# Norms, scaled keys and decays of a gated delta-rule pair of heads are made at the end of the pair ahead; two groups of small operations go from VectorE to ScalarE

## What is computed

```python
q, k = l2norm(q), l2norm(k)               # per head, after a short causal convolution and silu
gam = jnp.cumsum(chunks(g), axis=-1)       # log decay
decay = jnp.exp(jnp.where(tril_incl, gam[..., :, None] - gam[..., None, :], -jnp.inf))
kk = jnp.einsum('bhnid,bhnjd->bhnij', k, k)
a_mat = jnp.where(tril_strict, beta[..., None] * kk * decay, 0.0)
sol = lax.linalg.triangular_solve(eye + a_mat, rhs, lower=True, unit_diagonal=True)
u, w = sol[..., :dv], sol[..., dv:]
def step(S, xs):                           # over the chunks
    u_c, w_c, qk_c, qd_c, kd_c, gl_c = xs
    v_new = u_c - w_c @ S
    o_c = qd_c @ S + qk_c @ v_new
    return S * gl_c + kd_c.T @ v_new, o_c
y = rms_norm(o, gdn_norm) * silu(z)        # then the output projection
```

## Time and profile before

| | |
|---|---|
| three runs | 2388.29, 2393.89, 2395.19 us; median 2393.89 us |
| profiled execution | 2386.92 us, its span 2385.1 us |
| TensorE busy in the span | 2271.2 us, 95% |
| VectorE, ScalarE, GpSimd busy | 1202.6, 996.0, 1128.9 us |
| delta-rule pairs, layer 0 | 121.9 to 447.5 us of the span |
| delta-rule pairs, layer 1 | 1299.5 to 1625.5 us of the span |
| TensorE idle in those two stretches | 56.2 us together |

### The profile page before, as it was taken

The page is one execution under the profiler, slowest core; times in us unless marked ns, Lnnn a source line. Parts: engine busy times, 40 slices in busy tenths (PEclk is TensorE's granted clock), DMA queues, the critical chain, the costliest instruction groups (busy, mean ns, idle before and its releaser), DMA issues.

```text
span 2385.1 us, 32695 instructions
## 1 busy us (share of the span) xinstructions
PE 2271.2 (95%) x12724; PEld 1854.7 (78%) x12724; DVE 1202.6 (50%) x2284; ACT 996.0 (42%) x2125; POOL 1128.9 (47%) x824
## 2 busy tenths in 40 slices
PE   6989997999999999999988999979999999999997
PEld 5677876788878888888766777867887888888886
DVE  4768778544442344440157778775445333444302
ACT  5545544455442333332265455445455224333222
POOL 4365366243345555554443564453443555555542
PEclk9999998999999999999989999989999999999998
DMA  4212111122233333333321111102222333333332
GB/s 138 62 45 58 54 47 39 52 74 75 72 87 97 97 93 97 97 97 98 97 63 58 45 54 54 56 26 67 76 76 67 96 97 93 96 97 96 97 97 84
DMA packets 98506, 183.34 MB, mean 77 GB/s; under 512 B 10928, under 2 KB 11056, under 8 KB 98224
## 3 DMA queue, kind: packets, MB, share of 16 engines
q1 hardware_dynamic: 98352, 181.26, 26.8%
HBM read 179.12 MB, written 2.10 MB: 76 GB/s over the span
## 4 chain that ended last, share of the span: by engine, by line
PE 83%; DVE 12%; ACT 4%; issue 1%; DMA 0%; POOL 0%; SPq 0%; DVEq 0%; ACTq 0%
PE bank L1311 80%; DVE left L1013 1%; PE bank L1377 1%; DVE conv_acc L861 1%; ACT w_hi L532 1%; DVE z_act L861 1%; DVE left L861 1%; PE bank L1606 1%; DVE ob_lo L858 1%; DVE packed_rows L858 1%; DVE decay L1047 1%; ACT v_b L543 1%; DVE best L1008 0%; DVE inv L1077 0%; DVE packed L1080 0%
## 5 line engine op out<-in xcount | busy, mean ns | idle before, releaser
L447 POOL TENSOR_TENSOR w_lo<-w_raw,w_hi 128x512 fp32r<-128x512 f32 x668 | 930.6, 1414 | 1159.2 <-ACT w_hi L532 1159.2
L1311 PE MATMUL bank<-xn_hi,w_hi 128*128 128x512 f32 x1936 | 785.5, 406 | 11.1 <-POOL w_lo L447 3.6
L1311 PE MATMUL bank<-xn_lo,w_hi 128*128 128x512 f32 x1936 | 781.5, 404 | 0.4 <-POOL xn_lo L509 0.4
L1311 PE MATMUL bank<-xn_hi,w_lo 128*128 128x512 f32 x1936 | 781.7, 404 | 0.0
L532 ACT ACTIVATE w_hi<-w_raw 128x512 fp32r<-128x512 f32 x668 | 384.8, 624 | 738.6 <-PE bank L1311 734.6
L1311 PEld LDWEIGHTS bank<-xn_hi,w_hi 128*128 128x128 f32 x1936 | 369.4, 191 | 93.4 <-issue 12.0
L1311 PEld LDWEIGHTS bank<-xn_lo,w_hi 128*128 128x128 f32 x1936 | 369.0, 191 | 78.7 <-issue 4.0
L1311 PEld LDWEIGHTS bank<-xn_hi,w_lo 128*128 128x128 f32 x1936 | 369.8, 191 | 75.8 <-issue 5.4
L858 DVE TENSOR_TENSOR residual<-residual,bank 128x512 f32<-128x512 f32 x32 | 22.0, 686 | 258.6 <-PE bank L1311 258.4
L1311 PE MATMUL bank<-mid_hi,w_hi 128*128 128x512 f32 x352 | 137.0, 389 | 0.0
L1311 PE MATMUL bank<-mid_hi,w_lo 128*128 128x512 f32 x352 | 137.0, 389 | 0.0
(11 more groups left out here) (251 smaller groups left out, 3344.2 us busy)
## 6 DMA issues: line engine op xcount, KB each, us to landing
w_raw<-w_tiles SPq DMA_DIRECT2D x668, 256.0 KB, 2.6
residual<-x_t SPq DMA_DIRECT2D x4, 512.0 KB, 5.2
out_t<-normalised SPq DMA_DIRECT2D x8, 256.0 KB, 2.1
rope<-rope SPq DMA_DIRECT2D x1, 1024.0 KB, 10.3
mats<-mats SPq DMA_DIRECT2D x1, 704.0 KB, 7.7
vecs_all<-vecs SPq DMA_DIRECT2D x1, 133.0 KB, 7.6
```

The lines of the kernel that those rows point to most:

```text
L447: nc.gpsimd.tensor_tensor(w_lo[j][:], w_raw[j][:], w_hi[j][:].bitcast(F32), ALU.subtract).then_inc(s_lo, 1)
L1311: return nc.tensor.matmul(out, lhsT, rhs, start=start, stop=stop)
```

## The change

The steps kt and gb of pair i+1, with all that hangs on them up to `k_b`, `k_dec` and the scaled decay (now the functions `head_...`), are issued at the end of pair i, around its output norm. Pair 0 still makes its own. The transposes and products of ot (`outputs`) of pair i are issued in pair i+1, after kk; those of pair 3 stay at its end. On VectorE the minimum of the decay and the `v_new` copies are gone: ScalarE does them, the first as Relu with the sign turned. `packed` is no longer in SBUF but in bank 7, `z_act` is made after the inverse of the small blocks and not before it, and the tables of fill and of convolution steps have other numbers.

```diff
+            def head_gate(l, i, s):
+                act.wait_ge(head_p.sem, head_p.after(t, f"gb{s}"))
+                for c in range(NC):
+                    last = nc.scalar.activation(decay[s][:, c, :], chunks(by[s])[:, c, :], ACT.Relu, bias=hcol[:, s, 3, c:c + 1], scale=-1.0)
...
+            def head_rest(l, i):   
+                act.wait_ge(head_v.sem, head_v.after(t, "vark"))
+                nc.scalar.activation(rinv[:, :, 1, :], rinv[:, :, 1, :], ACT.Sqrt).then_inc(head_a.step("sqrtk"), 1)
+                head_gate(l, i, 1)
+                for s in range(2):
+                    act.wait_ge(head_a.sem, head_a.after(t, f"ga{s}"))
+                    nc.scalar.activation(decay[s][:], decay[s][:], ACT.Exp, scale=-1.0).then_inc(head_a.step(f"exp{s}"), 1)
...
                 evac("T0_", t_m, by)
+                if i < PAIRS - 1:
+                    front(l, i + 1, 0, True, split_next=False)
...
+                    for s in range(2):
+                        act.wait_ge(gdn_p.sem, gdn_p.after(t, f"V{c}_{s}"))
+                        copy(v_new[s][:], chunks(bx[s])[:, c, :]).then_inc(gdn_a.step(f"V{c}_{s}"), 1)
...
+                if i < PAIRS - 1:
+                    head_squares(l, i + 1)
+                    head_gate(l, i + 1, 0)
                 act.wait_ge(gdn_v.sem, gdn_v.after(t, "ovar"))
                 nc.scalar.activation(ocol[:], ocol[:], ACT.Sqrt).then_inc(gdn_a.step("osqrt"), 1)
-                stages(f"O{NC - 1}_", "ot")
+                if i < PAIRS - 1:
+                    head_rest(l, i + 1)
...
-                        last = V.tensor_scalar(decay[s][:, c, :], chunks(by[s])[:, c, :], hcol[:, s, 3, c:c + 1], 0.0, ALU.subtract, ALU.min)
...
-                        V.tensor_copy(v_new[s][:], chunks(bx[s])[:, c, :]).then_inc(gdn_v.step(f"V{c}_{s}"), 1)
...
                 stages("ovar")
+                if i < PAIRS - 1:
+                    head_keys(l, i + 1)
                 dve.wait_ge(gdn_a.sem, gdn_a.after(t, "osqrt"))
                 V.reciprocal(ocol[:], ocol[:]).then_inc(gdn_v.step("orinv"), 1)
                 dve.wait_ge(gdn_v.sem, gdn_v.after(t, "orinv"))
                 for s in range(2):
                     tt_(o_s[s][:], chunks(bz[s]), over_free(ocol[:, s, :]), ALU.mult).then_inc(gdn_v.step(f"osc{s}"), 1)
...
+                    pe.wait_ge(head_v.sem, head_v.after(t, f"kb{s}"))
+                    if i > 0:
+                        pe.wait_ge(gdn_v.sem, gdn_v.after(t - 1, f"osc{s}"))
                     columns(bz[s], k_b[s]).then_inc(gdn_p.step(f"kbT{s}"), 1)
...
+                if i < PAIRS - 1:
+                    head_keys(l, i + 1)
+                    d.issue(dense_after["kt"])
+                    head_gates(l, i + 1)
```

More of the change, by code:

```diff
@@ L344, in hybrid_trunk @@
[L344 to L351, removed]
@@ new lines, in hybrid_trunk @@
+        tail_p = steps("tail_pe", two("ot"))
+        tail_v = steps("tail_dve", two("og"))
+        gdn_p = steps("gdn_pe", [m for st in STAGES if st not in ("start", "ot", "kt", "gb") for m in (["sub"] if st == "sub" else two(st))])
+        gdn_a = steps("gdn_act", two("kbT", "eg", "sqq") + ["qe"] + two("ztanh", "T0_")
+                      + [m for L in LV for m in two(f"P{L}_")] + two("vb", *[f"{w}{c}_" for c in range(NC) for w in ("V", "osq")]) + ["osqrt"])
+        gdn_v = steps("gdn_dve", two("at") + ["red0", "red1", "row"] + [m for j in range(SB - 1) for m in (f"col{j}", f"inv{j + 1}")] + ["whole"]
+                      + two("i0_", "qk", "zact") + [m for L in LOW for m in two(f"Y{L}_", f"U{L}_")] + two(f"U{LV[-1]}_")
+                      + [m for c in range(NC) for m in two(f"R{c}_", f"S{c}_") if m[:3] not in ("R0_", f"S{NC - 1}_")]
+                      + ["ovar", "orinv"] + two("osc"))
@@ L472, in mask @@
                         nc.gpsimd.tensor_tensor(mt[L % 2][s][:], a_t[s][:], mat4(M_LEVEL + L - FIRST), ALU.mult).then_inc(gdn_g.step(f"mt{L}_{s}"), 1)
[L474 to L479, removed]
+                if i == 0:
+                    head(l, i)
                 for s in range(2):
@@ L1103, in gdn @@
                     tt_(qk_t[s][:], chunks(bx[s]), decay[s][:], ALU.mult).then_inc(gdn_v.step(f"qk{s}"), 1)
-                dve.wait_ge(gdn_a.sem, gdn_a.after(t, "sqq1"))
-                V.tensor_scalar(rinv[:, :, 0, :], rinv[:, :, 0, :], 16 * EPS * HD, 64 * EPS * EPS * HD, ALU.mult, ALU.add).then_inc(gdn_v.step("qe"), 1)
-                stages("sub", "T0_")
+                for s in range(2):
+                    dve.wait_ge(gdn_a.sem, gdn_a.after(t, f"ztanh{s}"))
+                    stt(z_act[s][:], z_act[s][:], 1.0, z_raw[s][:], ALU.add, ALU.mult).then_inc(gdn_v.step(f"zact{s}"), 1)
+                if i > 0:
+                    front(l, i, 6, "silu", True)
+                if tile_of is None:
+                    front_start(l, i + 1)
+                stages(*STAGES[:STAGES.index("T0_") + 1])
                 for L in LOW:
```

273 lines of the change are left out of this document (162 added, 111 removed).

## The result

The changed kernel takes 2410.9 us (median of four runs, 2407.3 to 2411.7), the kernel before 2391.1 us in the runs beside it (2388.3 to 2395.2). The ratio is 1.0088, with a 95% interval from 1.0075 to 1.0101: slower by about 20 us. The forecast was 2402, slower by 8.

What follows compares the result with a forecast made beforehand. TensorE, busy 95% of the span, was taken as the bound, with idle time and clock changing. Two layers of 2.9+1.2 us gave +8.2, 2395 us profiled; referred to the median 7 us higher, 2402, range 2372 to 2415.

Steps and rivals of the forecast that it cites:

- The head of pairs 1 to 3: TensorE waits ahead of kbT for the moved head's chain: 1.6 us in pair 1, 2.5 in pairs 2 and 3.
- sub: At sub no wait for packed_rows (0.7 us): 2.3 us back in pairs 1 and 2, 3.1 in pair 3.
- Tile 2: Behind T0, TensorE newly waits for z_raw, which waits for z_act: 2.65 us in pairs 0, 1 and 2.
- Pair 0: Waits of 2.9 us for hcol, 0.9 at kk, 1.1 at T0; with tile 2, 7.6 against 6.5: +1.1 us.
- Pair 3: First t_m_both wait grows to 6.7 us; +1.5 us idle in all, less 2 us of half clock: -0.5 us.
- `v_new` at nothing: ScalarE's copies of v_new, at most 0.386 us against VectorE's 0.29, are covered by dense products and cost nothing.
- The sum: Per layer 1.1+0.7+1.6-0.5 = +2.9 us, plus 1.2 us for the clock, times two layers: +8.2 us.
- The rule on the table switch: Ahead of kbT, a drain of about 1.38 us follows each table load: wait 3.9 us, not 2.5; total 2410.
- dearer: Rival: pair 3's chain slips throughout, long waits drop the clock, +9 to 12 us a layer, 2414; chance 0.15.

Runs made afterwards that it cites:

- the last kernel: Changed kernel with z_act ahead of sub, Relu behind the roots, pair 3's spare work moved, twelve start products between pair 0's kt and gb: 2360.6 us, 0.9877.

## Why the prediction was right, and where its sizes were off

The direction was right: idle time moved to tile 2 and `kbT`, and more came than went. The size was not: 20 us where 8 were forecast, though inside the stated range of 2372 to 2415. The profiled execution was to take 2395 us and took 2407.3, 12 us more. The forecast for the median missed by 9 us only because the 7 us that it added for the distance between the two were 3.6 here, and that is luck. By its own steps:

- **The head of pairs 1 to 3.** 1.6 us in pair 1 and 2.5 in pairs 2 and 3; measured 1.7 and 2.64. Four Relu in a row took 1.2 us where I had 1.1, and moving them took 1.0 us off each wait.
- **sub.** No wait for `packed_rows`, 0.69 us for it: right. Its worth was not. In the kernel before this part alone costs 0.7%. It also left slack that nothing used: VectorE waited 4.6 us for sub in pair 2.
- **Tile 2.** 2.65 us six times, 15.9; measured 17.2 in six, from 2.1 to 3.4. The sum came out right partly by luck, for the mean of the earlier trace rows was the mean of another place. `z_act` there is not 1.47 us: the first of each two took 1.2 to 2.6 us in those six pairs, and in the four pairs where it took 1.9 us or more it ended 0.55 us into the pause that ScalarE's own wait for it had made.
- **Pair 0.** `hcol` 2.9, measured 2.9; T0 1.1, measured 1.2; kk 0.9, measured none; `v_b` 1.1 was not in the sum.
- **Pair 3** is the step that failed: "-0.5 us", of which +1.5 idle and "less 2 us for one long spell at half clock". The wait of 6.7 us for `t_m_both` came out at 6.8 in layer 0, but at 9.6 in layer 1, by the held `z_act`. With its head the idle time rose by 2.4 and 4.3 us, not 1.5. And the clock gave nothing back. It went from 0.88 to 0.85 and 0.87, and beyond the moved work the matmuls are busy for 2.1 us more in layer 0 and 0.6 less in layer 1: +1.5 us in sum, where the forecast had -4. One long wait did not save clock over two short ones.
- **`v_new` at nothing.** Right in the changed kernel (`v_b` 2.3 us in all, against 1.5), wrong in the kernel before, with 7.3 us more. The number of products behind V isn't the difference: by the two tables it is six or close to it in pairs 0 to 2 of both kernels. What differs is that the changed kernel has the tanh of those convolutions a stage sooner (`CONV_AT`: O0, O1 and O2 in place of R1, R2 and R3), ahead of the copy that holds it up in the other. No run moves that alone.
- **The sum.** Idle time in the pairs rose by 16.9 us; the forecast had 2 x (2.9+2) = 9.8. The clock cost 4.3; the forecast had 2 x (1.2-2) = -1.6. The two misses are 7.1 and 5.9 us. Pair 3 has 3.7 and 5.5 of them, 9.2 of 13.0.

The rule on the table switch weighed in the prediction did not hold here: `o_s` and `k_b` came when the load alone would have them, 2.64 us late and not 3.9. Of the rivals, *dearer* named pair 3's chain and 2414 us and was nearest in time (2411), but its steps did not slip one by one: one operation was held.

What is shown: that holds end with GpSimd's rows or at a pause in them (two pairs of runs, with and without a pause); that in the changed kernel the pause at tile 2 came from ScalarE's wait for `z_act` (its trace, and the run that takes this wait away); and that moving `z_act` alone, or pair 3's spare work alone, undoes the loss (0.9982 each). What is only argued: that the moved tanh is why `v_new` costs nothing in the changed kernel. What stays open: why VectorE sometimes gets in between two GpSimd operations (0.7 to 1.8 us) and sometimes not until the last of the row, as in pair 3 of the changed kernel, where the longer `z_act` took 1.75 us in layer 0 and 9.2 us in layer 1; and what set the clock.

## What to carry to other kernels

A mean from the trace holds for an operation where it stands: one with two operands in SBUF, moved beside another stretch of GpSimd's, took 0.7 or 10 us here, so look for GpSimd's pauses at the new place before the price goes into a sum. Each small relief shifts VectorE against GpSimd, and a gain of 1 us at one wait was paid with a hold of 7 us at the next; give such an operation a gap by order or by a wait on GpSimd. Where a part of a change gives slack, look for who can use it: here `z_act` fitted into the time that the shorter chain to sub had opened.

## What the runs showed of the hardware

A VectorE operation with both inputs in SBUF (128x512, 0.68 us undisturbed) lasted 7.2 to 10.0 us when it came upon a row of GpSimd operations without a gap, and ended 0.55 us behind the row or at its first pause; the GpSimd operations kept their 1.25 us each. Operations beside them with one input in PSUM (`qk_t`, 0.68 us) were not touched. In other places the same two kinds took turns, with up to 1.8 us for VectorE's and 1.5 us for GpSimd's. The Trainium skill (SBUF — State Buffer, Who interferes with whom) has a VectorE instruction with two SBUF inputs contend with a GpSimd instruction that reads SBUF, for a shared port pair that is an exclusive lock, and has issue order decide who blocks. The traces agree on who is touched. A hold over a row of eight GpSimd instructions (9.9 us) is longer than a wait for the one that was issued first.

The granted clock over pair 3 did not follow the longest wait in it: 0.88 with waits of up to 4.0 us, 0.85 and 0.87 with one of 6.8 or 9.6 us, 0.86 and 0.84 in the run with `z_act` ahead of sub, and 0.92 and 0.97 in the last kernel, where no wait of the pair is longer than 3.6 us in either of these two. What sets it is not shown.
